# One plain fp32 product a tile in place of two fp32r pieces when expert outputs return to their tokens

## Chip, cores and metric

The kernel runs on one core of one Trainium2 chip. The metric is the device time of one launch in microseconds (us). Beside it stands the span of a profiled execution, from its first to its last recorded instruction.

## What is computed

One inference step of a one-layer backbone over 384 tokens of width 1024: 128 of a prompt (one tile, tile 0) and 256 of a sample (tiles 1 and 2). A Fourier and retention mixer comes first, which the change does not touch. Behind it stands a mixture of 64 experts with top-8 routing and one shared expert, then the gated sum into x and a final norm. All of it is in fp32. Cut to what matters here:

```python
sh1, sc1, g1, sh2, sc2, g2 = jnp.split(silu(cond) @ w_ada + b_ada, 6)   # one set for the prompt, one for the sample
x = x + g1 * mixer(...)
h = rmsnorm(x, norm2_g) * (1.0 + sc2) + sh2
hid = silu(einsum('td,edf->tef', h, we_g)) * einsum('td,edf->tef', h, we_u)
routed = einsum('tef,efd->td', hid * combine[..., None], we_d)
shared = (silu(h @ ws_g) * (h @ ws_u)) @ ws_d
x = x + g2 * (routed + shared)
y = rmsnorm(x, final_norm_g)
```

## The kernel before

The 64 experts are worked off as 32 pairs, in an order made on the chip. Each pair has 128 slots, 64 an expert (in the last five pairs 96 and 32), and every slot holds one token. For a pair p:

- POOL gathers the 128 token rows by an indirect DMA out of `h2_rows` (`gather`, line 658). TensorE transposes them (1218 and 1221), ScalarE copies them to `xT`.
- SP's queue loads the expert weights, 6 MB a pair, into a ring of pieces: gate and up (508, 509, and in halves 515, 516 for the last pairs) and down (526). Each load waits until the pair that held its place is through (`pair_freed`).
- TensorE: `gate_up(p)` (1281), the transposes of the next pair's tokens, the slot table of pair p + 2 (1159 or 1259), the transposes of hid (1292), then four of the six return tiles of pair p - 1, `down(p)` (1306), and the other two return tiles (`scatter`, `scatter_tile`, 1322). A return tile is one of three token tiles by one of two halves of 512 channels: a matmul with `slotT`, the 0/1 matrix of slot against token, as weights, and the pair's output as moving data. In pairs 0 to 11 one of the tiles has the shared expert's product ahead of it in the same bank (1320).
- The pair's output leaves PSUM as two fp32r pieces: ScalarE copies it to `y_hi` (`outputs`, 1681), VectorE subtracts that from the bank and writes `y_lo` (`remainder`, 2307). fp32r is fp32 data that the matmul takes in a shortened form; `slotT` has this type too. The tile is the sum of two matmuls, with `y_hi` and with `y_lo`.
- VectorE forms hid (2290), finds the slots of pair p + 2 (`picks`, 2203 to 2207) and adds the six tiles to the sums `hT` (`sums`, 2301).

The waits are written out by hand, as counts on semaphores: `hi_ready` and `lo_ready` count the pieces, `scattered` the return tiles done, `summed` the tiles added.

The last two pairs, 30 and 31, go another way (1383). The rows of g2 that belong to each slot's kind (prompt or sample) are gathered by POOL into `slot_gate` (`gather_gates`, 674); VectorE multiplies the down product by it (`remainder_gated`, 2317), ScalarE copies the product to `y_hi` (1693), VectorE forms `y_lo` (2322). Both pairs add into the same six banks. Meanwhile VectorE multiplies the sums of pairs 0 to 29 by g2 (`gate_sum`, 2376) and adds them to x (`add_sum`, 2380), so that the end is only `x += bank` (`last_sums`, 2427), the sums of squares on ScalarE (1724), and the norm (2477). SP's queue fetches g2's prompt row (621) and x's prompt tile (622), ahead of the last down weights.

```python
for n, y in enumerate((y_hi, y_lo)):
    ins = mm(o, slotT[k][:, t * P:(t + 1) * P], y[:, h * 512:(h + 1) * 512], start=(n == 0 and not shared), stop=(n == 1))
```

Of the kernel before, what the change touches and what calls it, by code (L numbers as in the profile page):

```python
# [8 lines left out]
F32R = mybir.dt.float32r  # L9
# [214 lines left out]
def trunk_kernel(nc, A, outs, consts, dists):  # L224
    y_prompt, y_sample, new_f, new_b = outs
    ctx = ExitStack()
    with ctx:
# [27 lines left out]
        idx = sb("idx", [P, KEEP + 3], I32)  # L255
# [105 lines left out]
        g2_rows = [U[:, 0:D], S0f]  # L361
# [20 lines left out]
        y_hi = within("y_hi", "Fm", 0, D)  # L382
        y_lo = within("y_lo", "Fm", D, D)
# [4 lines left out]
        y_gated = [QK[:, 1536:2048], AB1[:, 1024:1536]]  # L388
        slot_gate = {LAST - 2: AB1[:, 0:1024], LAST - 1: Fm[:, 2048:3072]}
        base_3 = small[:, 304:307]  # L390
        ssq_low = small[:, 307:310]

# [144 lines left out]
        def _(sp):  # L537
# [66 lines left out]
            for p in range(2, PAIRS):  # L604
                e = [sp.value_load(column(tab_order, 2 * p + n), min_val=0, max_val=E - 1) for n in range(2)]
                for n in range(2):
                    if p == 2 and n == 0:
                        sp.wait_ge(sem("x0_parked"), 16)
                        computed(sp, "h2T01")
                    else:  # L610
                        pair_freed(sp, PARTS * p + n)
                    if p < HALVED:
                        load_gate_up(sp, e[n] * P, p, n, f"gate_up_in{p % 3}")
                    else:
                        load_gate_up_half(sp, e[n] * P, p, n, 0, f"low_in{p % 2}")
                if p >= HALVED:
                    for n in range(2):
                        load_gate_up_half(sp, e[n] * P, p, n, 1, f"gate_up_in{p % 3}")
                if p == PAIRS - 1:
                    sp.wait_ge(sem("g2_stored"), 16)  # L620
                    sp.dma_start(g2_rows[0], mod_rows[MOD_AT["g2"], 0:1, :].broadcast_to([P, D])).then_inc(sem("first_tile_in"), 16)
                    sp.dma_start(x[:, 0, :], x0_rows).then_inc(sem("first_tile_in"), 16)
                pair_freed(sp, PARTS * p + 2)
                for n in range(2):
                    load_down(sp, e[n] * P, p, n, f"down_in{p % 3}")
                if p == 2:
                    computed(sp, "shT2")
                    sp.dma_start(sd_w[1], w_sd[:, 1, :]).then_inc(sem("shared_in"), 16)
# [33 lines left out]
        def _(pool):  # L662

            def gather_gates(p):

                if p == LAST - 2:
                    pool.wait_ge(sem("gate_up_done"), p)
                else:
                    pool.wait_ge(sem(f"gate_up_in{p % 3}"), 64 * (p // 3 + 1))
                pool.wait_ge(sem("scattered"), 72)  # L670
                pool.wait_ge(sem("slot_kinds"), p - (LAST - 3))
                stand_alone(pool, "pool_passed")
                n = KEEP + 1 + p % 2
                pool.indirect_dma_start(slot_gate[p], None, mod_rows[MOD_AT["g2"], :, :], bass.IndirectOffsetOnAxis(idx[:, n:n + 1], 0),
                                        bounds_check=1, oob_is_err=False).then_inc(sem("gates_in"), 16)
# [80 lines left out]
            for p in range(2, LAST):  # L756
# [24 lines left out]
        def _(pe):  # L781
# [513 lines left out]
            def down(p):  # L1295
                pe.wait_ge(sem("hidT_ready"), p + 1)
                pe.wait_ge(sem(f"down_in{p % 3}"), 32 * (p // 3 + 1))
                if p:
                    pe.wait_ge(sem("lo_ready"), 2 * p)
                else:  # L1300
                    last_in(2)
                    last_in(3)
# [7 lines left out]
            def scatter_tile(p, g, banks):  # L1310
# [10 lines left out]
                for n, y in enumerate((y_hi, y_lo)):  # L1321
                    ins = mm(o, slotT[k][:, t * P:(t + 1) * P], y[:, h * 512:(h + 1) * 512], start=(n == 0 and not shared), stop=(n == 1))  # L1322
# [36 lines left out]
            def scatter_duo_tile(halves, g):  # L1359
                t, h = g // 2, g % 2  # L1360
                for n, y in enumerate((y_hi, y_lo)):
                    ins = mm(ps[4 + g % 4][:, :], halves[h][:, t * P:(t + 1) * P], y[:, 0:512], start=(n == 0), stop=(n == 1))
                ins.then_inc(sem("scattered"), 1)

            def scatter(p, tiles):
                if 0 in tiles:
                    pe.wait_ge(sem("lo_ready"), 2 * (p + 1))
# [13 lines left out]
            def return_part(p, n, y, start, stop):  # L1381
                t, h = LAST_TILES[n]
                return mm(ps[LAST_BANKS[n]][:, :], slotT[p % KEEP][:, t * P:(t + 1) * P], y[:, h * 512:(h + 1) * 512], start=start, stop=stop)

            def scatter_next_to_last(tiles):
                p = LAST - 2
                if 0 in tiles:
                    pe.wait_ge(sem("summed"), 6 * p)
                    pe.wait_ge(sem("lo_ready"), 2 * p + 2)
                for n in tiles:  # L1390
                    if LAST_BANKS[n] == 1:
                        pe.wait_ge(sem("hidT_ready"), LAST)
                    return_part(p, n, y_hi, True, False)
                    return_part(p, n, y_lo, False, False).then_inc(sem("scattered"), 1)
# [38 lines left out]
            def further(q):  # L1433
# [9 lines left out]
                pe.wait_ge(sem("lo_ready"), p * 2)  # L1443
# [3 lines left out]
                pe.wait_ge(sem("lo_ready"), p * 2 + 2)  # L1447
# [22 lines left out]
        def _(act):  # L1470
# [205 lines left out]
            def outputs(p):  # L1676
                for h in range(2):
# [3 lines left out]
                    nc.scalar.copy(y_hi[:, h * 512:(h + 1) * 512], ps[2 + h][:, :]).then_inc(sem("hi_ready"), 1)  # L1681

            def outputs_duo(p):
                act.wait_ge(sem("down_done"), p * 2 + 2)
                act.wait_ge(sem("scattered"), p * 6)
                nc.scalar.copy(y_hi[:, 0:512], ps[2][:, :]).then_inc(sem("hi_ready"), 2)

            def outputs_gated(p):
                for h in range(2):
                    act.wait_ge(sem("y_gated"), 2 * (p - LAST + 2) + h + 1)  # L1690
                    if h == 0:
                        act.wait_ge(sem("scattered"), p * 6)
                    nc.scalar.copy(y_hi[:, h * 512:(h + 1) * 512], y_gated[h]).then_inc(sem("hi_ready"), 1)

            for p in range(LAST):
# [11 lines left out]
                if p in slot_gate:  # L1707
                    outputs_gated(p)
                else:
                    outputs(p)  # L1710
# [27 lines left out]
        def _(dve):  # L1738
# [462 lines left out]
            def picks(p, k, slotT_k, o_rank, slot_col):  # L2201
# [7 lines left out]
                if isinstance(p, int) and p in slot_gate:  # L2209
                    n = KEEP + 1 + p % 2  # L2210
                    v.tensor_scalar(idx[:, n:n + 1], idx_f[:, k:k + 1], float(CTX - T), None, ALU.is_ge).then_inc(sem("slot_kinds"), 1)
                    dve.wait_ge(sem("slot_kinds"), p - (LAST - 3))
# [90 lines left out]
            def remainder(p):  # L2303
                for h in range(2):
                    cut = slice(h * 512, (h + 1) * 512)
                    dve.wait_ge(sem("hi_ready"), p * 2 + (h + 1))
                    v.tensor_tensor(y_lo[:, cut], ps[2 + h][:, :], y_hi[:, cut], ALU.subtract).then_inc(sem("lo_ready"), 1)  # L2307

            def remainder_gated(p):
                j = p - (LAST - 2)  # L2310
                dve.wait_ge(sem("gates_in"), 16 * (j + 1))
                def gated(h):
                    cut = slice(h * 512, (h + 1) * 512)
                    dve.wait_ge(sem("down_done"), 2 * p + h + 1)
                    if j:
                        dve.wait_ge(sem("lo_ready"), 2 * p)
                    v.tensor_tensor(y_gated[h], ps[2 + h][:, :], slot_gate[p][:, cut], ALU.mult).then_inc(sem("y_gated"), 1)

                def low(h):
                    cut = slice(h * 512, (h + 1) * 512)  # L2320
                    dve.wait_ge(sem("hi_ready"), 2 * p + h + 1)
                    v.tensor_tensor(y_lo[:, cut], y_gated[h], y_hi[:, cut], ALU.subtract).then_inc(sem("lo_ready"), 1)

                gated(0)
                if j:
                    low(0)
                gated(1)
                if not j:
                    low(0)
                low(1)  # L2330
# [32 lines left out]
            def remainder_duo(p):  # L2363
                dve.wait_ge(sem("hi_ready"), p * 2 + 2)
                v.tensor_tensor(y_lo[:, 0:512], ps[2][:, :], y_hi[:, 0:512], ALU.subtract).then_inc(sem("lo_ready"), 2)

            tile_sums = [hTf[:, t * D:(t + 1) * D] for t in range(TT)]

            def gate_sum(n, t):
                if t == 0:  # L2370
                    dve.wait_ge(sem("first_tile_in"), 32)
                else:
                    dve.wait_ge(sem("g2_rows_in"), 16)
# [4 lines left out]
            def add_sum(n, t):  # L2378
                dve.wait_ge(sem("sum_gated"), n + 1)
                v.tensor_tensor(x[:, t, :], x[:, t, :], tile_sums[t], ALU.add).then_inc(sem("x_formed"), 1)  # L2380

            for p in range(PAIRS):
# [27 lines left out]
                if p in slot_gate:  # L2410
                    remainder_gated(p)
                else:
                    remainder(p)
# [17 lines left out]
            def further(q):  # L2431
# [11 lines left out]
                remainder_duo(p)  # L2443
# [67 lines left out]
```

## Time and profile before

| what | value |
|---|---|
| median of three runs | 893.12 us (890.53, 893.12, 894.96) |
| the profiled execution | 894.96 us, span 893.2 us |
| TensorE matmul busy | 869.7 us, 97% of the span |
| TensorE weight load busy | 444.6 us, 50% |
| VectorE busy | 471.7 us, 53% |
| ScalarE busy | 166.7 us, 19% |
| moved by DMA | 288.00 MB, mean 322 GB/s |

In rows of the trace PE is TensorE's matmul, PEld its weight load (beside PE), DVE VectorE, ACT ScalarE, POOL GpSimd, and SPq the SP engine's queue, which issues the weight loads. L1322 is line 1322 of the kernel. Matmuls are pipelined, so the duration of one overlaps the next: the pace is read from the distance of starts. A row `x6` of a timeline is six instructions merged, with their common time.

### The profile page before, as it was taken

The numbers are of one execution on the slowest core, as the hardware profiler recorded it, in microseconds if no ns is written. First come the engines' busy times: TensorE is split into PE (matmuls) and PEld (weight loads), VectorE is DVE, ScalarE is ACT, GpSimd is POOL, SyncE is SP. The second block draws the span as 40 slices with busy tenths as digits, with TensorE's granted clock in tenths as the row PEclk, the third lists the DMA queues.
The fourth block names the chain that finished last, engine by engine and source line by source line (L and its number), as shares of the span: only waits on it lengthen the run. The fifth ranks groups of instructions, "written<-read, shape, count | busy, mean of one in ns | idle before, by whom it ended". The sixth has DMA issues, their size and how long they took to land.

```text
span 893.2 us, 11423 instructions
## 1 busy us (share of the span) xinstructions
PE 869.7 (97%) x4186; PEld 444.6 (50%) x4186; DVE 471.7 (53%) x1030; ACT 166.7 (19%) x349; POOL 59.2 (7%) x76
## 2 busy tenths in 40 slices
PE   7999999999999999999999999999999999999993
PEld 6874445876655547654344444444444443444341
DVE  3645398936886945524354344544535344545455
ACT  4221012020000034121121211212121111212113
POOL 1020100000000000200000000000000000000000
PEclk9999999999999999999999999999999999999997
DMA  9998433512575857499999999999999999999992
GB/s 325 389 373 222 139 126 125 212 36 106 207 279 201 349 213 259 170 383 420 421 409 416 420 418 419 415 415 416 419 420 420 420 418 420 420 414 413 410 360 84
DMA packets 66074, 288.00 MB, mean 322 GB/s; under 512 B 6744, under 2 KB 6800, under 8 KB 43104
## 3 DMA queue, kind: packets, MB, share of 16 engines
q1 hardware_dynamic: 58480, 265.08, 75.1%
q0 software_dynamic: 7536, 22.16, 6.7%
q8 instruction: 35, 0.57, 0.3%
q14 instruction: 23, 0.19, 0.1%
HBM read 287.34 MB, written 4.33 MB: 327 GB/s over the span
## 4 chain that ended last, share of the span: by engine, by line
PE 92%; DMA 3%; DVE 2%; issue 2%; SPq 1%; ACT 1%; DVEq 0%; ACTq 0%
PE bank L1281 24%; PE bank L1306 12%; PE bank L854 12%; PE bank L1322 9%; PE bank L847 9%; PE bank L1071 5%; PE bank L1218 2%; DMA ring<-in_w_exp_up 2%; PE bank L1118 2%; PE bank L1221 1%; PE bank L859 1%; PE bank L864 1%; PE bank L1320 1%; PE bank L1292 1%; PE bank L1026 1%
## 5 line engine op out<-in xcount | busy, mean ns | idle before, releaser
L1281 PE MATMUL bank<-ring,QK 128*64 128x512 f32 (+1 forms) x1056 | 226.8, 595 | 1.8 <-DMA ring<-in_w_exp_up 1.8
L2301 DVE TENSOR_TENSOR hT<-bank,hT 128x512 f32<-128x512 f32 x174 | 109.6, 684 | 82.8 <-PE bank L1322 81.9
L1281 PEld LDWEIGHTS bank<-ring,QK 128*64 128x64 f32 (+1 forms) x1056 | 69.1, 128 | 124.9 <-issue 121.2
L1306 PE MATMUL bank<-ring,VG 128*64 128x512 f32 (+1 forms) x512 | 103.8, 611 | 3.2 <-issue 2.7
L2290 DVE SCALAR_TENSOR_TENSOR VG<-VG,cw,bank 128x256 f32<-128x256 f32 x32 | 15.4, 481 | 167.8 <-issue 161.2
L854 PE MATMUL bank<-hT,ring 128*128 128x384 f32 x256 | 86.0, 489 | 0.0
L847 PE MATMUL bank<-ring,hT 128*128 128x512 f32 x192 | 82.7, 593 | 0.0
L1322 PE MATMUL bank<-y_hi,slotT 128*128 128x512 f32 x180 | 81.0, 450 | 0.0
L1322 PE MATMUL bank<-y_lo,slotT 128*128 128x512 f32 x180 | 71.1, 395 | 0.0
L1681 ACT CAST y_hi<-bank 128x512 fp32r<-128x512 f32 x60 | 32.3, 589 | 194.9 <-PE bank L1322 191.7
L854 PEld LDWEIGHTS bank<-hT,ring 128*128 128x128 f32 x256 | 47.8, 190 | 33.7 <-issue 2.4
L1306 PEld LDWEIGHTS bank<-ring,VG 128*64 128x64 f32 (+1 forms) x512 | 29.8, 132 | 62.6 <-issue 62.6
L847 PEld LDWEIGHTS bank<-ring,hT 128*128 128x128 f32 x192 | 36.4, 190 | 45.8 <-issue 45.8
L1281 PE MATMUL bank<-spare,QK 128*64 128x512 f32 x128 | 56.6, 595 | 0.0
L1322 PEld LDWEIGHTS bank<-y_hi,slotT 128*128 128x128 f32 x180 | 33.9, 188 | 30.5 <-issue 25.7
L1663 ACT ACTIVATE VG<-bank 128x256 f32<-128x256 f32 x32 | 12.3, 383 | 191.2 <-PE bank L1281 191.2
L1071 PE MATMUL bank<-ring,U 128*128 128x512 f32 x96 | 42.0, 593 | 0.0
L2307 DVE TENSOR_TENSOR y_lo<-bank,y_hi 128x512 fp32r<-128x512 f32 x60 | 38.4, 680 | 3.9 <-ACT y_hi L1681 3.9
L1322 PEld LDWEIGHTS bank<-y_lo,slotT 128*128 128x128 f32 x180 | 34.0, 189 | 7.8 <-issue 2.9
L1668 ACT COPY QK<-bank 128x512 f32<-128x512 f32 x62 | 33.3, 589 | 5.8 <-PE bank L1218 5.8
L658 POOL DMA_INDIRECT QK<-h_rows,idx x16 | 15.9, 991 | 218.1 <-DVE idx L2207 215.4
L658 POOL DMA_INDIRECT VG<-h_rows,idx x16 | 16.1, 1003 | 211.5 <-DVE idx L2207 197.3
(407 smaller groups left out, 951.3 us busy)
## 6 DMA issues: line engine op xcount, KB each, us to landing
ring<-in_w_exp_down SPq DMA_DIRECT2D x56, 1024.0 KB
ring<-in_w_exp_gate SPq DMA_DIRECT2D x48, 1024.0 KB, 10.2
ring<-in_w_exp_up SPq DMA_DIRECT2D x48, 1024.0 KB, 13.4
ring<-in_w_ada SPq DMA_DIRECT2D x12, 2048.0 KB, 12.2
ring<-in_w_in SPq DMA_DIRECT2D x9, 2048.0 KB, 17.9
spare<-in_w_exp_gate SPq DMA_DIRECT2D x8, 1024.0 KB, 7.3
spare<-in_w_exp_up SPq DMA_DIRECT2D x8, 1024.0 KB, 12.6
spare<-in_w_exp_down SPq DMA_DIRECT2D x8, 1024.0 KB
```

Source lines behind the costliest of these rows:

```text
L658: pool.indirect_dma_start(xg[n], None, h2_rows, bass.IndirectOffsetOnAxis(idx[:, k:k + 1], 0), bounds_check=T - 1, oob_is_err=False).then_ ...
L847: ins = mm(o[:, :], h[:, k, t * P:(t + 1) * P], w[:, k, :], start=(k == 0), stop=(k == KC - 1))
L854: ins = mm(o[:, 0:T], w[:, k, m * P:(m + 1) * P], rhs[:, k, :], start=(k == 0), stop=(k == kc - 1))
L1071: ins = mm(o[:, :], mergedT[:, k, t * P:(t + 1) * P], w[:, k, :], start=(k == 0), stop=(k == KC - 1))
L1118: ins = mm(o[:, 0:ED], hT[:, k, t * P:(t + 1) * P], w[:, k, :], start=(k == 0), stop=(k == KC - 1))
L1281: ins = mm(ps[0][rows, :], xT[:, k, rows], gate_up_of(p, n)[:, k, :, :], start=(k == 0), stop=(k == KC - 1))
L1306: ins = mm(ps[2 + h][rows, :], hidT[:, j, rows], down_of(p, n)[:, j, h * 512:(h + 1) * 512], start=(j == 0), stop=(j == 1))
L1322: ins = mm(o, slotT[k][:, t * P:(t + 1) * P], y[:, h * 512:(h + 1) * 512], start=(n == 0 and not shared), stop=(n == 1))
L1668: nc.scalar.copy(halves[n], ps[4 + n][:, :].rearrange("p (k s) -> p k s", k=4)).then_inc(sem("xT_ready"), 1)
L1681: nc.scalar.copy(y_hi[:, h * 512:(h + 1) * 512], ps[2 + h][:, :]).then_inc(sem("hi_ready"), 1)
L2301: v.tensor_tensor(into, o, into, ALU.add).then_inc(sem("summed"), 1)
L2307: v.tensor_tensor(y_lo[:, cut], ps[2 + h][:, :], y_hi[:, cut], ALU.subtract).then_inc(sem("lo_ready"), 1)
```

## The change

The two pieces become one plain fp32 tensor `y_out`, which ScalarE copies out of PSUM, and a return tile is one matmul; `slotT` becomes plain fp32 as well. VectorE's subtraction is gone, and who waited for `hi_ready` or `lo_ready` waits for `y_ready`. In the last two pairs VectorE writes the gated product straight to `y_out`. The slot gates are formed on VectorE from g2's two rows and the slots' kinds, at the ends of pairs 28 and 29, in place of the two indirect fetches. g2's prompt row comes to POOL's queue behind the gather of pair 4, into the place of `y_lo`. The fetch of x's prompt tile moves behind the last down weights in SP's queue, and the final norm's gain row has another wait ahead of it.

```diff
-            return nc.alloc_sbuf_tensor_at(name, [P, n], F32R, offset=home[of] + 4 * at)[:, :]
+            return nc.alloc_sbuf_tensor_at(name, [P, n], F32, offset=home[of] + 4 * at)[:, :]
...
-        g2_rows = [U[:, 0:D], S0f]
+        g2_rows = [Fm[:, D:2 * D], S0f]
...
-        y_hi = within("y_hi", "Fm", 0, D)
-        y_lo = within("y_lo", "Fm", D, D)
+        y_out = within("y_out", "Fm", 0, D)
...
-                if p == PAIRS - 1:
-                    sp.wait_ge(sem("g2_stored"), 16)
-                    sp.dma_start(g2_rows[0], mod_rows[MOD_AT["g2"], 0:1, :].broadcast_to([P, D])).then_inc(sem("first_tile_in"), 16)
-                    sp.dma_start(x[:, 0, :], x0_rows).then_inc(sem("first_tile_in"), 16)
                 pair_freed(sp, PARTS * p + 2)
                 for n in range(2):
                     load_down(sp, e[n] * P, p, n, f"down_in{p % 3}")
+                if p == PAIRS - 1:
+                    sp.dma_start(x[:, 0, :], x0_rows).then_inc(sem("first_tile_in"), 16)
...
-                if p in slot_gate:
-                    gather_gates(p)
-            pool.wait_ge(sem("y_gated"), 2)
+                if p == 4:
+                    pool.wait_ge(sem("tile_done"), TILE_AT["sg2"] + 1)
+                    pool.dma_start(g2_rows[0], mod_rows[MOD_AT["g2"], 0:1, :].broadcast_to([P, D])).then_inc(sem("g2_rows_in"), 16)
+            pool.wait_ge(sem(f"down_in{(LAST - 1) % 3}"), 32 * ((LAST - 1) // 3 + 1))
+            pool.wait_ge(sem("y_ready"), 2 * (LAST - 1))
...
-                for n, y in enumerate((y_hi, y_lo)):
-                    ins = mm(o, slotT[k][:, t * P:(t + 1) * P], y[:, h * 512:(h + 1) * 512], start=(n == 0 and not shared), stop=(n == 1))
+                ins = mm(o, slotT[k][:, t * P:(t + 1) * P], y_out[:, h * 512:(h + 1) * 512], start=(not shared), stop=True)
...
-                    tiles = range(3 * h, 3 * h + 3)
-                    pe.wait_ge(sem("hi_ready"), 2 * p + h + 1)
-                    for n in tiles:
-                        return_part(p, n, y_hi, False, False)
-                    pe.wait_ge(sem("lo_ready"), 2 * p + h + 1)
-                    for n in tiles:
-                        return_part(p, n, y_lo, False, True).then_inc(sem("scattered"), 1)
+                    pe.wait_ge(sem("y_ready"), 2 * p + h + 1)
+                    for n in range(3 * h, 3 * h + 3):
+                        return_tile(p, n, False)
...
-                    nc.scalar.copy(y_hi[:, h * 512:(h + 1) * 512], ps[2 + h][:, :]).then_inc(sem("hi_ready"), 1)
+                    nc.scalar.copy(y_out[:, h * 512:(h + 1) * 512], ps[2 + h][:, :]).then_inc(sem("y_ready"), 1)
...
+            def gates_of_slots(p):
+                j = p - (LAST - 2)
+                dve.wait_ge(sem("g2_rows_in"), 32)
+                dve.wait_ge(sem("scattered"), 72)
+                for c, op in enumerate((ALU.is_lt, ALU.is_ge)):
+                    v.tensor_scalar(slot_kinds[:, j, c:c + 1], idx_f[:, p % KEEP:p % KEEP + 1], float(CTX - T), None, op).then_inc(sem("slot_kinds"), 1)
+                dve.wait_ge(sem("slot_kinds"), 2 * (j + 1))
+                v.tensor_scalar(slot_gate[p], g2_rows[0], slot_kinds[:, j, 0:1], None, ALU.mult).then_inc(sem("gate_formed"), 1)
+                dve.wait_ge(sem("gate_formed"), 2 * j + 1)
+                v.scalar_tensor_tensor(slot_gate[p], g2_rows[1], slot_kinds[:, j, 1:2], slot_gate[p], ALU.mult, ALU.add).then_inc(sem("gate_formed"), 1)
+
+            def outputs_gated(p):
+                j = p - (LAST - 2)
+                dve.wait_ge(sem("gate_formed"), 2 * (j + 1))
                 for h in range(2):
                     cut = slice(h * 512, (h + 1) * 512)
                     dve.wait_ge(sem("down_done"), 2 * p + h + 1)
+                    dve.wait_ge(sem("scattered"), 6 * p)
+                    v.tensor_tensor(y_out[:, cut], ps[2 + h][:, :], slot_gate[p][:, cut], ALU.mult).then_inc(sem("y_ready"), 1)
...
                 if p in slot_gate:
-                    remainder_gated(p)
-                else:
-                    remainder(p)
+                    outputs_gated(p)
+                if n in slot_gate:
+                    gates_of_slots(n)
```

## Rows read from the trace of the kernel before

**Rows 1.** The page's slices of 22.3 us: DMA share and rate.

```profile
DMA  9998433512575857499999999999999999999992
GB/s 325 389 373 222 139 126 125 212 36 106 207 279 201 349 213 259 170 383 420 421 409 416 420 418 419 415 415 416 419 420 420 420 418 420 420 414 413 410 360 84
```

**Rows 2.** Stages: us, busy (count) PE PEld DVE ACT POOL, granted clock, DMA share, GB/s.

```profile
599.00:845.00 246.00, 246.00 (x1321) 103.64 (x1324) 113.64 (x245) 47.51 (x98) 16.81 (x17) 1.00 1.02 417
845.00:861.00 16.00, 14.06 (x114) 5.59 (x110) 4.50 (x10) 1.78 (x5) 0.00 (x0) 1.00 1.02 410
```

**Rows 3.** Waits from 390 us on: total us, times, longest.

```profile
PE bank L1306 <- issue: 2.7, 1, 2.7
...
PE bank L1281 <- DMA ring<-in_w_exp_up: 1.8, 1, 1.8
```

**Rows 4.** Timeline, TensorE, a pair without the shared product: start us, us, what.

```profile
584.36 7.09 PE L1281 MATMUL bank<-ring,QK 128*64 128x512 f32 x32
...
592.68 0.44 PE L1292 MATMUL bank<-consts_sb,VG 128*128 128x128 f32 x2
...
593.19 0.39 PE L1322 MATMUL bank<-y_lo,slotT 128*128 128x512 f32 x1
...
594.58 0.40 PE L1322 MATMUL bank<-y_lo,slotT 128*128 128x512 f32 x1
594.91 3.65 PE L1306 MATMUL bank<-spare,VG 128*64 128x512 f32 x16
598.49 0.50 PE L1322 MATMUL bank<-y_hi,slotT 128*128 128x512 f32 x1
...
599.62 0.65 PE L1281 MATMUL bank<-ring,QK 128*64 128x512 f32 x2
```

**Rows 5.** Timeline, TensorE, a pair with the shared product.

```profile
415.38 0.44 PE L1292 MATMUL bank<-consts_sb,VG 128*128 128x128 f32 x2
...
418.48 3.65 PE L1306 MATMUL bank<-ring,VG 128*64 128x512 f32 x16
```

**Rows 6.** Timeline, TensorE, the output projection's plain fp32 products.

```profile
299.74 4.46 PE L1071 MATMUL bank<-ring,U 128*128 128x512 f32 x10
```

**Rows 7.** Lines 1322 and 1320: count, duration in ns (min/median/max), first and last start.

```profile
L1322 PE MATMUL bank<-y_hi,slotT x180: 390/396/797, 400.0 to 860.4; 128*128 128x512 f32 x180
...
L1320 PE MATMUL bank<-Fm,MB x12: 590/592/697, 399.5 to 567.2; 128*128 128x512 f32 x12
```

**Rows 8.** Subtractions into y_lo, and VectorE's wait ahead of hid in a pair.

```profile
L2307 DVE TENSOR_TENSOR y_lo<-bank,y_hi x60: 678/680/691, 390.1 to 845.2; 128x512 fp32r<-128x512 f32 x60
...
622.49 0.48 DVE L2290 SCALAR_TENSOR_TENSOR VG<-VG,cw,bank 128x256 f32<-128x256 f32 x1 [5.28 <-issue]
```

**Rows 9.** Timeline of the end, all engines.

```profile
848.58 2.12 SPq L621 DMA_DIRECT2D U<-mod_rows  x1
...
853.27 2.10 SPq L526 DMA_DIRECT2D ring<-in_w_exp_down  x2
...
860.94 7.07 PE L1281 MATMUL bank<-ring,QK 128*32 128x512 f32 x64
...
866.63 1.22 DVE L2380 TENSOR_TENSOR x<-x,hT 128x1024 f32<-128x1024 f32 x1
...
873.88 5.19 PE L1306 MATMUL bank<-ring,VG 128*32 128x512 f32 x32 [2.66 <-issue]
...
877.48 0.69 DVE L2317 TENSOR_TENSOR QK<-bank,Fm 128x512 f32<-128x512 f32 x1 [4.92 <-PE bank L1306]
...
882.04 2.50 DVE L2427 TENSOR_TENSOR x<-bank,x 128x512 f32<-128x512 f32 x4 [0.51 <-issue]
...
885.05 0.16 DVE L2417 TENSOR_SCALAR small<-small 128x3 f32<-128x3 f32 x1
885.12 0.68 DVE L2427 TENSOR_TENSOR x<-bank,x 128x512 f32<-128x512 f32 x1
...
888.80 1.28 DVE L2477 SCALAR_TENSOR_TENSOR x<-x,small,AB 128x1024 f32<-128x1024 f32 x1
```

More of the change, by code:

```diff
@@ L8 @@
 BF16 = mybir.dt.bfloat16
-F32R = mybir.dt.float32r
 I32 = mybir.dt.int32
@@ L254, in trunk_kernel @@
         cbf = sb("cbf", [P, 2, P], BF16)
-        idx = sb("idx", [P, KEEP + 3], I32)
+        idx = sb("idx", [P, KEEP + 1], I32)
         idx_f = sb("idx_f", [P, KEEP + 1])
@@ L391, in trunk_kernel @@
         ssq_low = small[:, 307:310]
+        slot_kinds = small[:, 310:314].rearrange("p (j c) -> p j c", c=2)
         R = DTf.rearrange("p (n c e) -> p n c e", n=8, c=TT)
@@ L1298, in down @@
                 if p:
-                    pe.wait_ge(sem("lo_ready"), 2 * p)
+                    pe.wait_ge(sem("y_ready"), 2 * p)
                 else:
@@ L1360, in scatter_duo_tile @@
                 t, h = g // 2, g % 2
-                for n, y in enumerate((y_hi, y_lo)):
-                    ins = mm(ps[4 + g % 4][:, :], halves[h][:, t * P:(t + 1) * P], y[:, 0:512], start=(n == 0), stop=(n == 1))
+                ins = mm(ps[4 + g % 4][:, :], halves[h][:, t * P:(t + 1) * P], y_out[:, 0:512], start=True, stop=True)
                 ins.then_inc(sem("scattered"), 1)
@@ L1366, in scatter @@
                 if 0 in tiles:
-                    pe.wait_ge(sem("lo_ready"), 2 * (p + 1))
+                    pe.wait_ge(sem("y_ready"), 2 * (p + 1))
                     if p:
@@ L1379, in scatter, with return_tile @@
                     scatter_tile(p, g, FREE_FIRST)
-            def return_part(p, n, y, start, stop):
+            def return_tile(p, n, first):
                 t, h = LAST_TILES[n]
-                return mm(ps[LAST_BANKS[n]][:, :], slotT[p % KEEP][:, t * P:(t + 1) * P], y[:, h * 512:(h + 1) * 512], start=start, stop=stop)
+                ins = mm(ps[LAST_BANKS[n]][:, :], slotT[p % KEEP][:, t * P:(t + 1) * P], y_out[:, h * 512:(h + 1) * 512], start=first, stop=(not first))
+                ins.then_inc(sem("scattered"), 1)
             def scatter_next_to_last(tiles):
@@ L1388, in scatter_next_to_last @@
                     pe.wait_ge(sem("summed"), 6 * p)
-                    pe.wait_ge(sem("lo_ready"), 2 * p + 2)
+                    pe.wait_ge(sem("y_ready"), 2 * p + 2)
                 for n in tiles:
@@ L1392, in scatter_next_to_last @@
                         pe.wait_ge(sem("hidT_ready"), LAST)
-                    return_part(p, n, y_hi, True, False)
-                    return_part(p, n, y_lo, False, False).then_inc(sem("scattered"), 1)
+                    return_tile(p, n, True)
             def scatter_last():
@@ L1442, in further @@
                 pe.wait_ge(sem("hidT_ready"), p + 1)
-                pe.wait_ge(sem("lo_ready"), p * 2)
+                pe.wait_ge(sem("y_ready"), p * 2)
                 pe.wait_ge(sem("down_next"), q * 32 + 32)
@@ L1446, in further @@
                 down_duo()
-                pe.wait_ge(sem("lo_ready"), p * 2 + 2)
+                pe.wait_ge(sem("y_ready"), p * 2 + 2)
                 pe.wait_ge(sem("summed"), p * 6)
@@ L1685, in outputs_duo @@
                 act.wait_ge(sem("scattered"), p * 6)
[L1686 to L1693, printed above, removed]
+                nc.scalar.copy(y_out[:, 0:512], ps[2][:, :]).then_inc(sem("y_ready"), 2)
             for p in range(LAST):
@@ L1706, in _ @@
                     shared_T(2)
-                if p in slot_gate:
-                    outputs_gated(p)
-                else:
+                if p not in slot_gate:
                     outputs(p)
@@ L2208, in picks @@
                 dve.wait_ge(sem("slots_ready"), p + 1)
[L2209 to L2212, printed above, removed]
             cnt = rg[0:E, 256:257]
@@ L2304, in remainder @@
+            def outputs_gated(p):
+                j = p - (LAST - 2)
+                dve.wait_ge(sem("gate_formed"), 2 * (j + 1))
                 for h in range(2):
                     cut = slice(h * 512, (h + 1) * 512)
[L2306 to L2313, printed above, removed]
-                    dve.wait_ge(sem("down_done"), 2 * p + h + 1)
[L2315 to L2330, printed above, removed]
@@ L2361, in hidden_duo @@
                 ins.then_inc(sem("hid_ready"), 1)
-            def remainder_duo(p):
-                dve.wait_ge(sem("hi_ready"), p * 2 + 2)
-                v.tensor_tensor(y_lo[:, 0:512], ps[2][:, :], y_hi[:, 0:512], ALU.subtract).then_inc(sem("lo_ready"), 2)
             tile_sums = [hTf[:, t * D:(t + 1) * D] for t in range(TT)]
             def gate_sum(n, t):
[L2370 to L2373, printed above, removed]
                 if n == 0:
@@ L2379, in add_sum @@
                 dve.wait_ge(sem("sum_gated"), n + 1)
+                if t == 0:
+                    dve.wait_ge(sem("first_tile_in"), 16)
                 v.tensor_tensor(x[:, t, :], x[:, t, :], tile_sums[t], ALU.add).then_inc(sem("x_formed"), 1)
@@ L2410, in _ @@
                 if p in slot_gate:
-                    remainder_gated(p)
-                else:
-                    remainder(p)
+                    outputs_gated(p)
+                if n in slot_gate:
+                    gates_of_slots(n)
             def base():
```

13 lines of the change are left out of this document (removed).

## The prediction, made before the change was run

> **What bounds the kernel now.** I read the slices first. From the nineteenth slice to the thirty-eighth, which lie in the stage of the 32 expert pairs, the transfers stand at 409 to 421 GB/s with the 16 DMA engines busy throughout [rows 1], and TensorE has its full clock of 2.4 GHz (1.00 in the stages [rows 2]). So two resources look full, and the question is which one sets the pace. The stages give the same picture with numbers: in the 246 us from 599 to 845 TensorE is busy 246.00 us and the DMA share is 1.02 [rows 2]. The waits decide between them. Of the whole time from 390 us on, TensorE's matmuls wait for a transfer once for 1.8 us and stand once more, ahead of the last down product, for 2.7 us [rows 3]; the profile names nothing for the second, and I read it as a transfer too, since the down weights that the product needs were issued only at 853.27, at the end of a full queue [rows 9]. TensorE is therefore the bound of the pair stage, and the transfers follow at almost the same rate. A change that makes TensorE slower costs its full price there; one that makes it faster would gain next to nothing.
>
> Then the timeline of one pair. A pair without the shared expert's product takes 599.62 - 584.36 = 15.26 us [rows 4], and in it TensorE never stands: gate and up products, transposes, four of the six tiles of the pair before returned, the down product, two more tiles. The return is what the change touches. Between 593.19 and 594.58 there are six starts of y_hi or y_lo products, so one takes 0.232 us and a tile (hi and lo) 0.464 us [rows 4].
>
> **Products, the main term.** The change removes two products of reduced fp32 (type fp32r) a tile and adds one of plain fp32 with the same 128x128 weights and 128x512 moving data. The fp32 product is in the trace in other places, and I price it from there.
> - A plain fp32 matmul stands in the trace as two records: the six shared products out of Fm (pairs 0, 2 to 10) are six calls in the code and 12 records, while every y_hi call is one record, 180 of them for 30 pairs of six tiles [rows 7].
> - Undisturbed, ten such records of the same shape (128x128 weights, 128x512) take 4.46 us, the last 0.59 of its own: (4.46 - 0.59) / 9 = 0.430 us a record, 0.86 us a product [rows 6].
> - In the very place of the change: from the transposes of hid to the down product a pair with one shared product takes 418.48 - 415.38 = 3.10 us [rows 5], one without it 594.91 - 592.68 = 2.23 us [rows 4]: 0.87 us for one fp32 product between return tiles.
> I take 0.858, between a pure stream at the gate products' pace (7.0 us for 32 records, two side by side, hence 0.43 to 0.44 a record [rows 4]) and the other two. So a tile costs 0.858 - 0.464 = 0.394 us more, and not less, although there is one instruction in place of two.
>
> The trace thus shows that the fp32 product costs nearly four times the fp32r one (0.858 against 0.232). The Trainium skill's FP8 and Floating Point Precision (TensorE Precision Notes) says that reduced fp32 is read and truncated and true fp32 makes four passes through the array; by that rule, the trace agrees. Its TensorE: Matmul & The Clock Gate (Weight-path perf modes) says that the array takes one element per cell and cycle whatever the element's width; read as holding for fp32 too, the product would cost a single pass and the change would win, which is the first rival below.
>
> For the 30 pairs returned ahead of the last pair's gate product: 180 x 0.394 = 70.9 us. All of it is on TensorE, which is busy without a gap, so nothing covers it.
>
> **What else the pair loses, on covered engines.** ScalarE's copies stay (60 of 0.588 us, now to plain fp32). VectorE loses 60 subtractions of 0.680 us [rows 8], 1.3 us a pair. TensorE waited for neither, so this is worth 0 in the pairs. With pairs of 15.26 + 6 x 0.394 = 17.6 us, the transfers have slack: the 1.8 us wait of the second to last gate product goes [rows 3], -1.8 us.
>
> **The g2 row of the prompt at pair 4.** One 512 KB transfer leaves SP's queue near the end, where its issue held the queue for 2.12 us ahead of the last down weights [rows 9], and comes to POOL's queue behind the gather of pair 4. Behind it there is the gather for pair 5, which has a whole pair of time. Below: 0. Above: 2.1 us of held queue, if the gather of pair 5 were late; I take 0, since TensorE gains 2.4 us a pair of slack against every transfer.
>
> **Slot gates on VectorE.** They replace two indirect fetches. Each costs two one-column operations (0.16 us by the nearest row, 128x3), a scaling of 128x1024 and a combination of 128x1024; the nearest rows are the 128x1024 product and sum, 1.22 us, and the final scale with two factors, 1.28 us [rows 9]. Twice 0.32 + 1.22 + 1.28 = 5.6 us at the ends of pairs 28 and 29. What covers it: there VectorE stands 5.28 us in a pair before it can form hid [rows 8], and a set of gates needs 2.8 us. If that cover were gone, at most 5.6 us. I take 0. Both one-column compares move out of the slot search, -0.3 us, covered as well.
>
> **The prompt's x tile last.** It goes from before the last down weights to behind them: with both transfers gone from ahead of them, the down weights are issued when their place is free, not after the 4.7 us from 848.58 to 853.27 in which SP's queue issued those two [rows 9]. x's tile is wanted only at its sum, behind the last gate product. 0 for itself; the waiting time it frees is in the tail's sum.
>
> **The tail.** Let G be the start of the last pair's gate product, 860.94 before [rows 9]. After: G = 860.94 - 1.8 + 70.9 = 930.0. Before, the next-to-last pair's tiles ended where the 2.66 us idle began, 873.88 - 2.66 = 871.22, so G + 10.28; six tiles more at 0.394 make G + 12.64. There the weights have long landed. The down product then takes 3.58 us as in a pair [rows 4], not 5.19 at a clock that had fallen in the idle time [rows 9]: G + 16.2. VectorE's gated output writes y_out itself (0.69 us a half), so the ScalarE copy and the subtraction go out of the chain; the first half is ready at G + 15.2, ahead of TensorE, and the second at G + 17.0, under the first three products. Six products of 0.858: G + 21.4. The last sum, 0.16 later and 0.68 long: G + 22.2. From the last sum's end (885.80) to the last scale's end (890.08) it was 4.28 us, and 3.12 from there to the end of the span [rows 9]; these stay: G + 29.6, where it was 32.26 before. The tail gives back 2.7 us.
>
> **Sum.** 930.0 + 29.6 = 959.6 us span, against 893.2: +66.4. The profiled execution took 894.96, 1.76 more than its span, and 1.84 more than the median of 893.12. So 961.4 on its own account and 959.6 at the median: I say 960.
>
> **Rivals.**
> - **The fp32 product is cheap here.** Speaks for it: one instruction replaces two, and the kernel loses 62 steps of VectorE. If a product cost no more than 0.232 us, a pair would need 13.9 us of TensorE, and the transfers would set the pace: they already run at 417 GB/s. Then only the 1.05 MB of gathered gates (2.5 us at that rate) leaves the transfers, and the tail's copy and subtraction go (the sums would start at 873.88 + 5.19 + 0.69 + 0.51 = 880.3, not at 882.04 [rows 9], 1.7 us): 893.1 - 4.2 = 889 us. It decides as soon as a product costs less than the 0.464 of the pieces. Against it: both places where the same shape runs in plain fp32 show 0.86 [rows 5, 6]. This is the side "not slower". Chance 0.03, two thirds of it within 0.5% of before.
> - **The products do not overlap.** If the two records of a product did not run into each other behind another bank's product, each would cost its whole 0.59 us [rows 6], a product 1.18, and 192 tiles another 192 x 0.32 = 62 us: 1022 us. Against it is the shared product's 0.87 in the same stream. Chance 0.03.
> - **A new wait takes over in the longer pairs.** VectorE's gates delay hid of pairs 30 and 31, or the last norm's gain row lands late: up to 5.6 us for the first, 966 us. It belongs to my range.
>
> **Chances and range.** The forecast, all 192 products at 0.85 to 0.87, has 0.94. Its own ends: 0.85 in place of 0.858 takes 1.5 us away and 0.87 adds 2.3; the tail is known to 3 us; gates in the open add 5.6; queue effects 2.1; the three runs lie 2.6 below and 1.8 above their median. Together 951 to 970, which needs neither rival. A measurement of this kernel can tell 0.5% (4.5 us) from no change. Slower 0.97, same 0.02, faster 0.01.
>
> **What would show it.** In the profile after: 360 records of the return product in the pair stage, starts 0.43 us apart; a pair of 17.6 us; TensorE still without gaps; DMA share under 1, near 365 GB/s; no wait for a transfer in the last three pairs; down of pair 31 in 3.6 us. I am wrong if the starts are 0.23 apart, if TensorE stands for y_ready or hid_ready in each pair, or if the stage up to 373 us has moved.

## The result and the profile after

The kernel after the change takes 961.22 us (median of five runs, 959.98 to 961.45) against 893.05 us for the one before: a ratio of 1.0767, 95% interval 1.0744 to 1.0789. The profiled execution took 961.37 us with a span of 959.6 us. The prediction said 960 us, and a span of 959.6.

The page's slices, as in [rows 1], and below them the costliest groups (line, engine, operation, count, busy us and mean ns, idle before and what ended it):

```profile
DMA  9998227023948575999999899899999998989951
GB/s 334 389 368 206 95 88 275 23 88 136 332 171 352 215 256 199 399 376 369 379 380 367 349 378 381 331 390 391 364 390 382 365 385 358 383 313 352 358 225 69
...
L2267 DVE TENSOR_TENSOR hT<-bank,hT 128x512 f32<-128x512 f32 x174 | 117.9, 690 | 139.6 <-PE bank L1306 135.4
L1306 PE MATMUL bank<-y_out,slotT 128*128 128x512 f32 x360 | 168.6, 601 | 0.0
```

A stage of the kernel after, in the columns of [rows 2]:

```profile
650.00:910.00 260.00, 260.00 (x1220) 95.51 (x1220) 91.56 (x195) 42.48 (x88) 14.83 (x15) 1.00 0.93 367
```

TensorE is as full as it was, 260.00 of 260 us, at the same granted clock of 1.00. The transfers are not: from 1.02 and 417 GB/s they fall to 0.93 and 367 GB/s. A pair still moves the same bytes; the pairs became longer. The return products have 360 records where there were 180 of y_hi and 180 of y_lo, so the count is the same and only the pace differs. VectorE's sums now wait 135.4 us in all for the products, where they waited 81.9 before.

One pair of the kernel after, TensorE's timeline, to be laid beside [rows 4]:

```profile
630.60 7.09 PE L1266 MATMUL bank<-ring,QK 128*64 128x512 f32 x32
...
638.92 0.44 PE L1277 MATMUL bank<-consts_sb,VG 128*128 128x128 f32 x2
...
639.19 3.60 PE L1306 MATMUL bank<-y_out,slotT 128*128 128x512 f32 x8
...
642.72 3.65 PE L1291 MATMUL bank<-ring,VG 128*64 128x512 f32 x16
...
646.31 1.98 PE L1306 MATMUL bank<-y_out,slotT 128*128 128x512 f32 x4
...
648.22 2.37 PE L1266 MATMUL bank<-ring,QK 128*64 128x512 f32 x10
```

From gate product to gate product it is 648.22 - 630.60 = 17.62 us, where [rows 4] have 15.26. Everything but the return keeps its length: the gate product 7.09 us, the down product 3.65. From the transposes of hid to the down product it was 2.23 us and is 642.72 - 638.92 = 3.80; the two later tiles with their step to the next gate product took 599.62 - 598.49 = 1.13 us and take 648.22 - 646.31 = 1.91. That is 1.57 + 0.78 = 2.35 us more, for six tiles 0.39 each.

The end of the kernel after, all engines, beside [rows 9]:

```profile
911.69 0.43 SPq L621 DMA_DIRECT2D x<-x_rows  x1
...
913.17 0.20 DVE L2274 TENSOR_SCALAR small<-idx_f 128x1 f32<-128x1 f32 x2
...
913.41 0.75 DVE L2276 TENSOR_SCALAR Fm<-Fm,small 128x1024 f32<-128x1024 f32 x1
...
914.20 1.28 DVE L2278 SCALAR_TENSOR_TENSOR Fm<-S,small,Fm 128x1024 f32<-128x1024 f32 x1
...
920.07 0.48 DVE L2256 SCALAR_TENSOR_TENSOR VG<-VG,cw,bank 128x256 f32<-128x256 f32 x1 [4.38 <-issue]
...
929.96 7.08 PE L1266 MATMUL bank<-ring,QK 128*32 128x512 f32 x64
...
942.53 3.64 PE L1291 MATMUL bank<-ring,VG 128*32 128x512 f32 x32
...
946.10 5.42 PE L1366 MATMUL bank<-y_out,slotT 128*128 128x512 f32 x12
...
955.21 1.28 DVE L2426 SCALAR_TENSOR_TENSOR x<-x,small,AB 128x1024 f32<-128x1024 f32 x1
```

The last down product starts without a wait and takes 3.64 us, not 5.19; the twelve records behind it take 5.42 us without a gap, and the whole end from 942.53 on is 17.1 us where it was 893.2 - 873.88 = 19.3. The slot gates cost VectorE 0.20 + 0.75 + 1.28 = 2.23 us a pair, and behind the set shown here it still stands 4.38 us ahead of hid.

### The profile page after: what moved, and what is told of

Same layout as the page of the kernel before. It is cut to its first block, busy times and chain, and to the rows that moved or that the text cites. A ratio compares the mean times of both kernels' runs of the same rounds, so it can differ in the third digit from the quotient of the medians.

```text
span 959.6 us, 11355 instructions
## 1 busy us (share of the span) xinstructions
PE 942.8 (98%) x4186; PEld 445.3 (46%) x4186; DVE 445.7 (46%) x972; ACT 164.3 (17%) x345; POOL 57.6 (6%) x75
## 4 chain that ended last, share of the span: by engine, by line
PE 95%; DMA 2%; DVE 1%; issue 1%; SPq 0%; ACT 0%; DVEq 0%
PE bank L1266 23%; PE bank L1306 17%; PE bank L1291 12%; PE bank L839 11%; PE bank L832 9%; PE bank L1056 4%; DMA ring<-in_w_ada 2%; PE bank L1203 2%; PE bank L1103 2%; PE bank L1206 1%; PE bank L1277 1%; PE bank L844 1%; PE bank L1366 1%; PE bank L849 1%; PE bank L1305 1%; PE bank L1011 1%
## 5 line engine op out<-in xcount | busy, mean ns | idle before, releaser
L2267 DVE TENSOR_TENSOR hT<-bank,hT 128x512 f32<-128x512 f32 x174 | 117.9, 690 | 139.6 <-PE bank L1306 135.4
L1306 PE MATMUL bank<-y_out,slotT 128*128 128x512 f32 x360 | 168.6, 601 | 0.0
L1306 PEld LDWEIGHTS bank<-y_out,slotT 128*128 128x128 f32 x360 | 64.0, 190 | 82.0 <-issue 75.8
L1660 ACT COPY y_out<-bank 128x512 f32<-128x512 f32 x60 | 32.3, 589 | 263.4 <-PE bank L1306 260.1
L654 POOL DMA_INDIRECT VG<-h_rows,idx x16 | 16.1, 1003 | 244.9 <-DVE idx L2177 244.9
L1056 PEld LDWEIGHTS bank<-ring,U 128*128 128x128 f32 x96 | 18.0, 190 | 22.1 <-issue 21.9
L1735 DVE SCALAR_TENSOR_TENSOR AB<-ring,condr,AB 128x512 f32<-128x512 f32 x35 | 26.3, 752 | 1.2
L2173 DVE TENSOR_SCALAR slotT<-bank,consts_sb 128x384 f32<-128x384 f32 x32 | 19.8, 617 | 15.1 <-PE bank L1144 13.0
```

Of the source, the lines that this page charges most:

```text
L654: pool.indirect_dma_start(xg[n], None, h2_rows, bass.IndirectOffsetOnAxis(idx[:, k:k + 1], 0), bounds_check=T - 1, oob_is_err=False).then_ ...
L1056: ins = mm(o[:, :], mergedT[:, k, t * P:(t + 1) * P], w[:, k, :], start=(k == 0), stop=(k == KC - 1))
L1306: ins = mm(o, slotT[k][:, t * P:(t + 1) * P], y_out[:, h * 512:(h + 1) * 512], start=(not shared), stop=True)
L1660: nc.scalar.copy(y_out[:, h * 512:(h + 1) * 512], ps[2 + h][:, :]).then_inc(sem("y_ready"), 1)
L1735: ins = v.scalar_tensor_tensor(part, w[:, k, :], condr[:, k, c:c + 1], part, ALU.mult, ALU.add)
L2173: v.tensor_scalar(slotT_k, o_rank, cols[:, slot_col:slot_col + 1], None, ALU.is_equal).then_inc(sem("slot_found"), 1)
```

## Experiments

The theory: the loss is the pace of the plain fp32 product, times 192, on an engine that has no gap; the rest of the change is covered. The rivals: the loss comes from the other parts (gates, rows, waits); a plain product costs because it stands alone among others, not by streaming; the transfers set the pace already, or a chain over VectorE and ScalarE does.

**The product's type alone, in the kernel after.** One fp32r product a tile.

```diff
-            return nc.alloc_sbuf_tensor_at(name, [P, n], F32, offset=home[of] + 4 * at)[:, :]
+            return nc.alloc_sbuf_tensor_at(name, [P, n], mybir.dt.float32r, offset=home[of] + 4 * at)[:, :]
```

> The kernel after with y_out and slotT as fp32r again, so that a return tile is one fp32r product (the low piece of the expert output is left out, the tile is less exact). My theory: the whole loss is the 0.858 us of a plain product against 0.464 us of the two pieces, and the pair stage of before was set by TensorE with the transfers close behind. A tile is now 0.232 us, TensorE needs 13.9 us a pair, and the transfers at about 417 GB/s become the bound: pairs of 15.1 to 15.7 us, about 885 us, TensorE waiting for weights in the later pairs. Rival A, TensorE alone sets the pace: 893 - 192 x 0.232 = 848 us and no waits. Rival B, the loss came from the gates, the rows or the waits of the change and not from the product's type: over 940 us.

Measured: 888.74 us (four runs), ratio to before 0.9947, interval 0.9927 to 0.9967. One type in the kernel after takes back the whole loss and 4 us more, with gates, rows and waits unchanged: rival B is out. It does not take back what TensorE saved. The waits of this run from 390 us on, in the columns of [rows 3]:

```profile
PE bank L1266 <- DMA ring<-in_w_exp_up: 28.9, 17, 2.9
...
PE bank L1266 <- DMA spare<-in_w_exp_up: 5.8, 3, 2.5
```

And its stage from 600 to 800 us, in the columns of [rows 2]:

```profile
600.00:800.00 200.00, 178.87 (x832) 73.10 (x836) 74.83 (x168) 36.72 (x76) 12.90 (x13) 0.97 1.01 419
```

From 390 us on TensorE stands for weights 20 times, 34.7 us in all, while the transfers go on at 419 GB/s with a share of 1.01; its granted clock falls to a mean of 0.97 in this stage (1.00 in the kernel before), which costs some of what the product saves as well. That is rival A's end: the kernel before lay only a few us above the transfers' own time.

When the waits begin says more. Gate products of this run, the first in an early pair, the second with the first wait for weights, the third sixteen pairs later:

```profile
450.30 7.09 PE L1266 MATMUL bank<-ring,QK 128*64 128x512 f32 x32
...
524.72 7.09 PE L1266 MATMUL bank<-ring,QK 128*64 128x512 f32 x32 [0.74 <-DMA ring<-in_w_exp_up]
...
782.45 7.09 PE L1266 MATMUL bank<-ring,QK 128*64 128x512 f32 x32 [1.86 <-DMA ring<-in_w_exp_up]
```

For ten pairs there is no wait for weights: TensorE lives off what the ring holds. From then on a pair takes (782.45 - 524.72) / 16 = 16.1 us, and that is the transfers' pace. The kernel before had the same 419 GB/s between 600 and 800 us and pairs of 15.26 us. So it used its weights a little faster than they came, and could do so to the end of the 32 pairs only because of what the ring held at their start.

**Both pieces as plain fp32, in the kernel before.**

```diff
-            return nc.alloc_sbuf_tensor_at(name, [P, n], F32R, offset=home[of] + 4 * at)[:, :]
+            return nc.alloc_sbuf_tensor_at(name, [P, n], F32, offset=home[of] + 4 * at)[:, :]
```

> The kernel before with both pieces and slotT as plain fp32: two plain products a tile, everything else as before (the low piece is then zero). My theory, price by type and product: 2 x 0.858 = 1.716 us a tile against 0.464, 192 x 1.252 = 240 us more, less 4 us of transfer waits that go: about 1130 us, pairs of 22.8 us. Rival, what costs is a plain product among others once a tile (a switch of type or bank, the longer weight load), and not its own streaming: about 960 to 970 us.

Measured: 1126.46 us (two runs), ratio 1.261, interval 1.2586 to 1.2635. TensorE's timeline of this run, four return tiles of one pair:

```profile
612.29 1.02 PE L1322 MATMUL bank<-y_hi,slotT 128*128 128x512 f32 x2
613.15 1.02 PE L1322 MATMUL bank<-y_lo,slotT 128*128 128x512 f32 x2
...
618.30 1.02 PE L1322 MATMUL bank<-y_lo,slotT 128*128 128x512 f32 x2
619.25 3.65 PE L1306 MATMUL bank<-ring,VG 128*64 128x512 f32 x16
```

Each product is two records now, and seven products lie between 612.29 and 618.30: 0.859 us each. By that price the pairs' 384 products add 384 x (0.859 - 0.232) = 241 us, and the run is 234 us longer; most of the difference is what the kernel before loses by its transfer waits and the fallen clock at the end (1.8, 2.7 and 1.6 us in its profile), of which this run has nothing. The cost follows the number of plain products; a fixed cost of a single one among others is out.

**The other parts alone, with the pieces kept.** The kernel before, with gates on VectorE, x's tile last and g2's row by POOL (into its old place, so it can come only after pair 27). SP's queue is changed as in the diff of the change.

```diff
+                if p == 29:
+                    pool.wait_ge(sem("down_done"), 56)
+                    pool.dma_start(g2_rows[0], mod_rows[MOD_AT["g2"], 0:1, :].broadcast_to([P, D])).then_inc(sem("g2_rows_in"), 16)
-                if p in slot_gate:
-                    gather_gates(p)
...
+                if n in slot_gate:
+                    gates_of_slots(n)
```

> The kernel before with the two fp32r pieces kept, and the other parts of the change made: slot gates formed on VectorE, x's prompt tile last, g2's prompt row out of SP's queue (here into its old place behind the gather of pair 29). My theory: these parts are covered and take 1.05 MB and two queue places from ahead of the last down weights, so the wait ahead of the last down product falls from 2.7 us to under 1 and the clock stays up there: 886 to 890 us. Rival, the parts cost something where the transfers have no slack (gates on VectorE delay hid of pairs 30 and 31 by up to 2.3 us each, g2's row delays weights): 893 to 898 us.

Measured: 890.82 us (12 runs), ratio 0.9976, interval 0.9963 to 0.9989. The parts are a small gain where the transfers are tight, 1.9 us; the time lies just above the 886 to 890 us that I expected. TensorE goes into the last down product without a wait in this run, and at a granted clock of 1.00 the product takes 3.64 us:

```profile
871.68 3.64 PE L1293 MATMUL bank<-ring,VG 128*32 128x512 f32 x32
875.62 0.96 PE L1370 MATMUL bank<-y_hi,slotT 128*128 128x512 f32 x3 [0.30 <-ACT y_hi L1680]
...
877.60 0.96 PE L1370 MATMUL bank<-y_hi,slotT 128*128 128x512 f32 x3 [0.29 <-ACT y_hi L1680]
```

**The order of the queues alone.** As the last, but POOL still gathers the gates: only the moved fetches of x's tile and of g2's row are left of the edit.

> The kernel before with only the order of the queues changed: x's prompt tile behind the last down weights in SP's queue, g2's prompt row in POOL's queue behind the gather of pair 29; slot gates still gathered by POOL (two transfers of 512 KB). My theory: what e3_pieces_kept won (0.9976 of before) is the two queue places and the 1.05 MB of gates in front of the last down weights. With the gates still gathered, the first fetch lies ahead of those weights and costs its 1.3 us of transfer: 891 to 893 us, a wait of 1 to 2 us ahead of the last down product. Rival, the queue places are all of it: 890 to 891 us and no wait ahead of the last down product, as in e3_pieces_kept.

Measured: 892.78 us (12 runs), ratio 1.0004, interval 0.9988 to 1.002. So the two queue places give nothing that can be measured, and what the version before it won belongs to the gates' 1.05 MB or to their fetches; the two intervals just touch, and no run separates the bytes from the fetches. The time is as I expected, the reason is not: in its trace there is no wait ahead of the last down product. The wait in the gate product of pair 30 is 1.7 us, as it was in the kernel before (1.8 us), and 0.9 us with the gates on VectorE.

**The last pair returned by plain products, all others by pieces.** On top of the version with the pieces kept; the gated output is written by VectorE straight to the tensor that TensorE reads.

```diff
-                        return_part(p, n, y_hi, False, False)
...
-                        return_part(p, n, y_lo, False, True).then_inc(sem("scattered"), 1)
+                        ins = mm(ps[LAST_BANKS[n]][:, :], slotT_last[:, t * P:(t + 1) * P], y_out[:, hh * 512:(hh + 1) * 512], start=False, stop=True)
+                        ins.then_inc(sem("scattered"), 1)
```

> As e3_pieces_kept, and the last pair alone returned by one plain fp32 product a tile, its gated output written by VectorE straight to y_out. My theory: in the tail the pieces' chain (gate, copy, subtract) is longer than the six plain products; from the start of the last down product to the end it was 17.1 us in the kernel after and is 17.7 us with pieces at full clock, so this is 0 to 1 us faster than e3_pieces_kept: 886 to 889 us. Rival, the products' 6 x 0.394 = 2.4 us more are all on the path: 1 to 2.4 us slower than e3_pieces_kept.

Measured: 890.67 us (seven runs), ratio 0.9967, interval 0.9953 to 0.998; that is above the 886 to 889 us I gave, and beside 0.9976 the two can't be told apart. In the traces the end is shorter, from the last down product to the end of the span 886.9 - 869.88 = 17.0 us against 889.9 - 871.68 = 18.2:

```profile
869.88 3.64 PE L1295 MATMUL bank<-ring,VG 128*32 128x512 f32 x32
873.45 5.42 PE L1391 MATMUL bank<-Fm,MB 128*128 128x512 f32 x12
```

The twelve records have no gap here, while the pieces stand twice for ScalarE's copy. But the profiled execution of this version (888.79 us) lies below its median, that of the version with pieces alone (891.71 us) above its own, and the medians show nothing of this 1.2 us. In this one place, where nothing else is left for TensorE, the plain product is at least no loss. The two versions with pieces and with the gates on VectorE are 2 to 3 us faster than the kernel before, and so some 70 us faster than the kernel after.

**Fewer bytes, with one fp32r product a tile.** From pair 5 on only half of each expert's down weights is loaded; for the other half the products read what lay in the ring, so this version, like the next, leaves out part of the work.

```diff
+            if isinstance(p, int) and 5 <= p < PAIRS:
+                w, src = w[:, 0:CELL // 2], src[:, 0:CELL // 2]
             sp.dma_start(w, src).then_inc(sem(landed), 16)
```

> As e1_one_piece (a tile is one fp32r product, the low piece left out), and from pair 5 on only half of each expert's down weights is loaded (1 MB a pair left out; the other half of the products' weights is what lay in the ring). It tells what held e1_one_piece at 889 us. My theory: the transfers; 5.5 MB a pair at 418 GB/s are 13.2 us, under TensorE's 13.9 us, so now TensorE sets the pace: no waits for weights, pairs of 13.9 us, 843 to 850 us. Rival, a chain over VectorE and ScalarE (sums before a bank is free, hid before its transpose) held the pairs at 15.5 us: no change, 885 to 889 us.

Measured: 846.10 us (three runs), ratio 0.9486, interval 0.9472 to 0.95. Of two down products in its timeline, a pair apart:

```profile
701.95 3.65 PE L1293 MATMUL bank<-ring,VG 128*64 128x512 f32 x16
...
715.82 0.65 PE L1293 MATMUL bank<-ring,VG 128*64 128x512 f32 x2
```

715.82 - 701.95 = 13.87 us: the pair is 15.26 - 6 x 0.232, to the last digit. No gate or down product waits for weights any more. So it was the transfers that held the one-piece version at 16.1 us a pair (I had 15.5, which only its shortest pairs take), and no chain over VectorE or ScalarE.

**Fewer bytes, with the pieces of before.** The same edit in the kernel before.

> The kernel before with the same half of the down weights left out from pair 5 on. If TensorE set the pace of the pairs of before, as I said in the prediction, they stay at 15.26 us, and only the transfer waits of the end go: 1.8 us, 2.7 us and the 1.6 us of the fallen clock: 886 to 888 us. Rival, the transfers already set the pace of before (its pairs merely look full): 855 to 875 us.

Measured: 888.51 us (five runs), ratio 0.9966, interval 0.9953 to 0.9978, a little above the 888 I gave as the upper end. The stage from 600 to 800 us:

```profile
600.00:800.00 200.00, 200.00 (x964) 84.93 (x964) 92.08 (x199) 38.03 (x79) 12.88 (x13) 1.00 0.95 361
```

With a sixth of the bytes gone, the kernel before gains 3.9 us, while the one-piece version gained 42.6. TensorE did set the pace of before, with the transfers right behind: relieving either alone gains 4 us, relieving both 46.

**The cover of the slot gates, in the kernel after.** Each pair's gates are formed three times.

```diff
+                for again in range(3):
                     v.tensor_scalar(slot_gate[p], g2_rows[0], slot_kinds[:, j, 0:1], None, ALU.mult).then_inc(sem("gate_formed"), 1)
...
```

> The kernel after with each pair's slot gates formed three times (2 x 2 more pairs of operations of 0.75 and 1.28 us, 4.1 us more at the end of pairs 28 and 29, same result). I gave the gates a price of 0 because VectorE stands idle ahead of hid; in the kernel after it still stands 4.38 us there at pair 30. My theory: the cover holds, 0 to 0.5 us, 961 us. Rival, the gates are on the path of hid: 4 to 8 us slower, 965 to 969 us.

Measured: 960.75 us (four runs), ratio to before 1.0768, interval 1.0753 to 1.0784, the same as the kernel after. But the cover is used up. VectorE at the end of pair 29:

```profile
919.06 1.28 DVE L2279 SCALAR_TENSOR_TENSOR Fm<-S,small,Fm 128x1024 f32<-128x1024 f32 x1
920.43 0.29 DVE L2295 SCALAR_TENSOR_TENSOR VG<-consts_sb,expert_at,VG 128x64 f32<-128x64 f32 x1
920.64 0.08 DVE L2295 DVE_READ_ACCUMULATOR VG<-consts_sb,expert_at,VG 128x1 f32 x1
920.76 0.48 DVE L2256 SCALAR_TENSOR_TENSOR VG<-VG,cw,bank 128x256 f32<-128x256 f32 x1
```

There is no idle time left ahead of hid (it was 4.38 us), and TensorE waits for it 0.2 us.

## Why the prediction was right

- **What bounds.** Two resources looked full, and I gave the pace to TensorE because it hardly ever waited. Shown: half the down bytes gave 3.9 us with the pieces and 42.6 with one piece. That a faster product would gain next to nothing is shown too: the one-piece version gained 4.0 us of the 44.5 that 192 x 0.232 would make, and 1.9 us is what the other parts gain alone. What I had wrong here is "at almost the same rate": the transfers alone need 16.1 us a pair, more than the 15.26 of TensorE, and only the weights already in the ring hid it through 32 pairs. For the change, with pairs of 17.6 us, it made no difference.
- **The product.** I took 0.858 us from three rows elsewhere in the trace. A pair after is 17.62 us; I had 17.6. The three prices I had, 0.86 undisturbed, 0.87 in place and the gate products' pace, were all the same thing. (Between 593.19 and 594.58 lie seven starts, not six; the six distances give the 0.232 all the same.)
- **The start of the last gate product.** 929.96, where I had 930.0. In this lies 0.28 us by which the whole pair stage began later (the first gate product at 373.77, at 373.49 before), so the term for the 180 tiles was some 0.4 us too large, and the two errors nearly cancel. That the span agrees to 0.1 us is luck to this extent. The 1.8 us wait is gone, as I had it.
- **The gates.** Priced at 2.8 us a set, measured 2.23: the scaling of 128x1024 by one factor takes 0.75 us, not the 1.22 of a product of two tensors. At 0 on the path; tripled, TensorE waits 0.2 us in the trace, and the median shows nothing.
- **g2's row, x's tile.** No transfer wait stands in the last pairs of the kernel after. My reason for a gain from x's tile (the down weights are issued sooner) shows no gain where it could count: the order alone gave 1.0004. Here it did not matter, since the longer pairs had removed the wait already.
- **The tail.** G + 12.57 for the last down product (I had 12.64), 3.64 us for it, and G + 29.64 for the end of the span (29.6).
- **From the span to the median.** The profiled execution took 961.37 us, and the sum gives 961.4. From this I took another 1.84 us, because the profile of before lay that much above its median, and said 960. That step failed: the profile of the kernel after lies only 0.15 us above its own median of 961.22. The two transfer waits and the fallen clock, which the profile of before shows, I had taken off already.
- **The range.** The ends that I listed add up to 952.9 and 974.8, not to 951 and 970. The measured time lies in both.
- **The rival with the cheap product.** For a product of 0.232 us I worked out 889 us, held by the transfers; the run with one fp32r product took 888.74. The bound was right; the agreement to 0.3 us is luck, since the way there (ten pairs without a wait, then 16.1 us each) is in none of its terms. What kept the change from that time was the type and nothing else.

What stays open: what the last down product of the kernel before waits for, and in which executions. The prediction took it for a transfer at the end of a full queue. The profile of before, TensorE alone (us, busy, granted clock, DMA share, GB/s):

```profile
871.20:873.88 2.68, 0.02 (x1) 0.96 0.18 72
873.88:875.50 1.62, 1.62 (x8) 0.50 0.07 23
```

The queue is no longer full during the wait, with a share of 0.18; if a transfer is waited for, it is one of the last few still under way, and no view names it. The second row shows the fallen clock with which the product begins. The order of the queues removes this wait in its own trace and does not change the median. The mean granted clock of every execution gives a hint: of the 19 of the kernel before measured beside the first experiments, the three at 0.992 took 894.65 to 895.52 us and the four at 0.996 took 890.89 to 892.37 us. So the longer ones lose clock somewhere; whether they lose it here would take several profiles of the same kernel to tell.

## What to carry to other kernels

Count an edit of matmuls in the time their type takes, not in instructions: two fp32r products that carry a plain fp32 one in pieces cost 0.464 us, the one product 0.858, and on an engine without gaps that is the whole result. Before making the busiest engine faster, look at the second: here a tile at half the price gained 4 us of the 44.5 that it saved, since the transfers were full too. An engine that does not wait is no proof that its supply keeps up. It may live off a stock, and a run in which it asks for more shows when the stock ends (here after ten pairs). Work that leaves an engine with slack (the subtractions, 1.3 us a pair of VectorE) is worth nothing by itself.

## What the runs showed of the hardware

With 128x128 weights and 512 columns at the full clock, an fp32r product took 0.232 us and a plain fp32 product 0.858 us, and the plain one stands in the trace as two records. Its price was the same in three surroundings: 0.859 us in a stream of eight, and 0.86 and 0.87 in the two places of [rows 5, 6].

The rate of the transfers was less firm. The one-piece version with half of each down load, between 600 and 800 us:

```profile
600.00:800.00 200.00, 198.53 (x1087) 76.34 (x1084) 84.44 (x189) 42.63 (x88) 13.87 (x14) 1.00 1.00 393
```

The DMA share was 1.00 at 393 GB/s, while the version with whole down loads stood at 1.01 with 419 GB/s. A full share is thus no fixed rate. The halved loads have rows of 4 KB where they were 8 KB, but no run here shows whether that is the reason.
